# The memory's norm in a PSUM bank, and the low part of a unit of weights in one GpSimd operation

## What is computed

```python
def layer_norm(x, g, b):
    mu = jnp.mean(xf, -1, keepdims=True)
    var = jnp.mean(jnp.square(xf - mu), -1, keepdims=True)
    return ((xf - mu) * lax.rsqrt(var + LN_EPS) * g + b).astype(x.dtype)
...
mem_n = layer_norm(mem, mem_ln_g, mem_ln_b)
...
mk, mv = jnp.split(mem_n @ w_mem_kv[i], 2, axis=-1)
```

## Time and profile before

| what | value |
| --- | --- |
| median of 3 runs | 1919.36 us (1918.63 to 1919.83) |
| the profiled execution's own time | 1918.94 us |
| its span | 1917.1 us |
| TensorE (PE) busy | 1867.1 us, 97% |
| TensorE weight loads (PEld) | 1529.6 us, 80% |
| GpSimd (POOL) busy | 1517.8 us, 79% |
| ScalarE (ACT) busy | 945.5 us, 49% |
| VectorE (DVE) busy | 805.3 us, 42% |
| low parts on GpSimd (L1183) | 1242 operations, 1476.8 us |
| high parts on ScalarE (L1211) | 624 operations, 616.3 us |

### The profile page before, as it was taken

How to read it: one execution, slowest core, us unless ns; L and a number is a source line. 1 busy time by engine, 2 the same in 40 slices (tenths; PEclk the granted TensorE clock), 3 DMA queues, 4 the chain that set the end, 5 groups by cost and what they waited for, 6 DMA issues and landing times.

```text
span 1917.1 us, 27395 instructions
## 1 busy us (share of the span) xinstructions
PE 1867.1 (97%) x9610; PEld 1529.6 (80%) x9610; DVE 805.3 (42%) x1929; ACT 945.5 (49%) x1501; POOL 1517.8 (79%) x1330
## 2 busy tenths in 40 slices
PE   7999999999999999999999999999999999999999
PEld 6778888877888887788888678887787887788877
DVE  6784110446311155411146741106757445455534
ACT  3554444354444355444435644434656654555743
POOL 6768989884897977698987779797686887777785
PEclk9999999999999999999999999999999999999999
DMA  8454656563766554465655456655564564555453
GB/s 274 132 153 149 194 154 232 180 194 102 208 196 214 176 187 139 145 189 147 238 161 149 153 163 186 196 195 166 173 181 130 157 205 153 164 170 176 132 175 110
DMA packets 184557, 330.54 MB, mean 172 GB/s; under 512 B 12220, under 2 KB 44520, under 8 KB 184424
## 3 DMA queue, kind: packets, MB, share of 16 engines
q1 hardware_dynamic: 176512, 323.21, 54.4%
q10 hardware_dynamic: 7912, 5.59, 1.0%
HBM read 325.35 MB, written 3.41 MB: 171 GB/s over the span
## 4 chain that ended last, share of the span: by engine, by line
PE 84%; POOL 5%; DVE 5%; DMA 2%; ACT 2%; issue 2%; SPq 0%; DVEq 0%; ACTq 0%
PE acc L1417 24%; PE acc L1418 23%; PE acc L1424 21%; POOL w_lo L1183 5%; PE tps L1364 4%; PE acc L1439 2%; PE acc L1420 2%; PE ops L1481 2%; PE tps L1457 2%; DMA raw<-in_w_down 1%; PE acc L1388 1%; PE acc L1390 1%; PE acc L1389 1%; DVE QT L1594 1%; PE ops L1376 1%
## 5 line engine op out<-in xcount | busy, mean ns | idle before, releaser
L1183 POOL TENSOR_TENSOR w_lo<-raw,w_hi 128x512 fp32r<-128x512 f32 (+2 forms) x1242 | 1476.8, 1226 | 358.8 <-ACT w_hi L1211 357.4
L1211 ACT CAST w_hi<-raw 128x1024 fp32r<-128x1024 f32 (+3 forms) x624 | 616.3, 991 | 745.7 <-PE acc L1424 560.4
L1417 PE MATMUL acc<-w_hi,xT_hi 128*128 128x512 f32 (+1 forms) x1808 | 687.0, 384 | 4.9 <-ACT U L1245 3.0
L1418 PE MATMUL acc<-w_lo,xT_hi 128*128 128x512 f32 (+1 forms) x1808 | 667.5, 373 | 0.0
L1424 PE MATMUL acc<-w_hi,xT_lo 128*128 128x512 f32 (+2 forms) x1744 | 505.3, 371 | 0.0
L1417 PEld LDWEIGHTS acc<-w_hi,xT_hi 128*128 128x128 f32 x1808 | 341.8, 189 | 74.3 <-issue 14.5
L1418 PEld LDWEIGHTS acc<-w_lo,xT_hi 128*128 128x128 f32 x1808 | 342.4, 189 | 52.6
L1424 PEld LDWEIGHTS acc<-w_hi,xT_lo 128*128 128x128 f32 x1744 | 318.2, 189 | 58.4 <-DVE xT_lo L1694 1.2
L1754 DVE TENSOR_TENSOR H<-G,acc 128x512 f32<-128x512 f32 (+1 forms) x48 | 30.9, 643 | 332.7 <-PE acc L1424 332.7
L1417 PE MATMUL acc<-w_hi,hT_hi 128*128 128x512 f32 x352 | 139.6, 396 | 3.4 <-POOL w_lo L1183 3.4
L1418 PE MATMUL acc<-w_lo,hT_hi 128*128 128x512 f32 x352 | 137.3, 390 | 0.0
(11 more groups left out here) (209 smaller groups left out, 1998.8 us busy)
## 6 DMA issues: line engine op xcount, KB each, us to landing
raw<-in_w_gate_up SPq DMA_DIRECT2D x160, 512.0 KB, 4.0
raw<-in_w_in SPq DMA_DIRECT2D x104, 512.0 KB, 4.1
raw<-in_w_down SPq DMA_DIRECT2D x88, 512.0 KB, 4.1
raw<-in_w_out SPq DMA_DIRECT2D x48, 512.0 KB, 3.4
raw<-in_w_in_a SPq DMA_DIRECT2D x32, 512.0 KB, 3.9
raw<-in_w_in_b SPq DMA_DIRECT2D x20, 512.0 KB, 4.4
raw<-in_w_mem_kv SPq DMA_DIRECT2D x16, 512.0 KB, 4.1
raw<-in_w_gate_up SPq DMA_DIRECT2D x32, 256.0 KB, 2.8
```

Source lines behind the costliest of these rows:

```text
L1183: ins = nc.gpsimd.tensor_tensor(w_lo[:, r, i, 0:ch.width], raw[:, r, i, 0:ch.width], w_hi[:, slot, i, 0:ch.width].bitcast(F32), ALU.subtract)
L1211: nc.scalar.copy(w_hi[:, u.u % SPLIT, 0:u.nk, 0:u.chunk.width], raw[:, u.u % RAW, 0:u.nk, 0:u.chunk.width]).then_inc(S["hi_ready"], 1)
L1417: nc.tensor.matmul(o, hi[:, tok], wh, start=first_k, stop=False)
L1418: ins = nc.tensor.matmul(o, hi[:, tok], wl, start=False, stop=False)
```

## The change

Three things are edited.
- `low_part` on GpSimd: one operation over both k-tiles of the unit instead of one for each. It computes the same numbers, and raises the same semaphore once. The first unit's low part is made by VectorE, as before.
- The memory's norm: three operations for each half, through bank 1 of `ops`: `(m - mean) * r` into the bank, `* gain` in the bank, `+ bias` back into the rows. Before the first, VectorE waits for the release of the bank's last holder. The plan gives the task this room, and the half releases the bank itself.
- Costs in the plan: the low part 230 + 1.97 ns a column instead of 240 + 2.12 (for 1024 columns 2247 instead of 2411 ns), and a half of the memory's norm 2300 instead of 1600 ns.

```diff
             else:
-                u.low = self.task("POOL", "low", u, 240 + 2.12 * size, "lo_ready", [u.split])
+                u.low = self.task("POOL", "low", u, 230 + 1.97 * size, "lo_ready", [u.split])
...
                 one = p.stage(apply, fn, [gain.load, first, *also[t]], prio=t - 1 if fn == "rms_pre" else 0, half=half, **st)
                 halves.append(one)
+                if fn == "mem_norm":
+                    one.room, one.release, one.it.banks = ("ops", [(1,)]), one, [one]
...
-    norm_tiles("mem_norm", g, [[mem]] * T, "mem", scale=2500, acts="m")
+    norm_tiles("mem_norm", g, [[mem]] * T, "mem", scale=2500, apply=2300, acts="m")
...
                 pool.wait_ge(S["hi_ready"], u.split.n)
-                for i in range(u.nk):
-                    ins = nc.gpsimd.tensor_tensor(w_lo[:, r, i, 0:ch.width], raw[:, r, i, 0:ch.width],
-                                                  w_hi[:, slot, i, 0:ch.width].bitcast(F32), ALU.subtract)
-                ins.then_inc(S["lo_ready"], 1)
+                c = slice(0, ch.width)
+                nc.gpsimd.tensor_tensor(w_lo[:, r, 0:u.nk, c], raw[:, r, 0:u.nk, c], w_hi[:, slot, 0:u.nk, c].bitcast(F32),
+                                        ALU.subtract).then_inc(S["lo_ready"], 1)
...
                 elif fn == "mem_norm":
-                    m = rows("mem")[:, t, HALF[st.half]]
-                    norm_apply(t, m, m, halves(st.gain, st.half), done)
+                    m, (gg, bb) = rows("mem")[:, t, HALF[st.half]], halves(st.gain, st.half)
+                    mv, r = norm_columns(t, False)
+                    z = ops[:, st.banks[0].slot[0], :]
+                    for h in st.banks[0].held:
+                        dve.wait_ge(S[h.sem], h.n)
+                    link(v.tensor_scalar(z, m, mv[:, 0:1], r, ALU.subtract, ALU.mult))
+                    link(v.tensor_tensor(z, z, gg, ALU.mult))
+                    v.tensor_tensor(m, z, bb, ALU.add).then_inc(done, 1)
```

## The result

The changed kernel takes 1926.07 us (median of 6 runs, 1925.22 to 1927.53), the kernel before beside it 1919.59 (1917.43 to 1921.59): ratio 1.0036, interval [1.0023, 1.0049]. The profiled execution took 1925.97 us, its span 1924.1. The forecast was 1911.6, with 1905.0 to 1918.6: it missed on the far side; slower had been given a chance of 0.07.

What follows compares the result with a forecast made beforehand. TensorE, busy 97%, was taken as the bound, leaving its 50 us of standing to change. Terms -9.3 - 3.5 + 5 = -7.8 took 1918.94 to 1911.1; median 1911.6 us, range 1905 to 1918.6.

Steps and rivals of the forecast that it cites:

- Norm in a bank, -9.3: Memory's norm near 42 us: unheld bank operations let TensorE transpose earlier; 7.4 + 1.4 + 0.5 = 9.3 us gained.
- Low parts at the w_down starts, -3.5: At four w_down starts TensorE waits for low parts; merged units come 0.16 us sooner, 3.5 us gained, bounds 0 and 5.
- What the longer operation costs VectorE, +5: Held VectorE operations wait longer where VectorE leaves a GpSimd run early: 7.1 us at most, 5 taken.
- the list of places: Places said to cost: GpSimd runs at 1362.43, 1663.17 and 1681 us; 2.7 + 2.2 + 2.2 us at most.
- The condition of two tiles read from SBUF: From the norm's 8.76 us operation: a VectorE operation reading two SBUF tiles is held while GpSimd works.
- The price per hold: A held VectorE operation waits for 2.39 us of GpSimd instead of 1.30, up to 1.09 us more each.
- the argument of the run of fixed work: A GpSimd run is fixed work; operations held until its end finish as now, so longer operations add nothing there.
- the 450 us place: Two low parts at 450.57 us: the first held operation waits longer, the second not at all; they end as now.
- behind the latent: Six latent operations ahead of 1406 us grow up to 6.5 us, covered by idle VectorE; counted nothing, 2 if cover short.
- Order, 0 +- 3: New plan costs reorder all queues a little; no sign given, 3 us either way allowed.
- Rival 2: Every held operation on the path pays in full, 12 us in all, against gains of 12.8: 1918.6 us; chance 0.13.
- Rival 3: VectorE shut out through whole GpSimd runs at 1362, 1663, 1681 us and the latent: 22 us lost, 1928.5; chance 0.05.

Runs made afterwards that it cites:

- after: The changed kernel, with all three edits, measured beside the kernel before: 1926.07 us, ratio 1.0036.
- norm_one_op: Kernel before plus the norm in a bank and all low parts merged, in the order of the old low-part cost: 1918.45 us, ratio 0.9991.
- after_far: The changed kernel, its new order kept, with only the 34 units at held places split into two operations again: 1910.07 us, ratio 0.9952.
- one_op_far: norm_only with the low part merged for all units except the 34 at held places: 1903.02 us, ratio 0.9908.
- one_op_near: norm_only with the low part merged for only the 34 units at held places: 1925.59 us, ratio 1.0028.
- norm_only: The changed kernel with the old two-operation low part and its old plan cost, leaving the norm in a bank alone: 1909.73 us, ratio 0.9951.
- split_again: The changed kernel with the low part in two operations again, plan costs and order kept: 1914.76 us, ratio 0.9975.
- low_cost: The kernel before with only the plan's low-part cost changed to 230 + 1.97, so only the order differs: 1923.03 us, ratio 1.0017.
- one_low_op: The kernel before with only the low part merged into one operation, order unchanged: 1926.96 us, ratio 1.0037.

## Why the prediction was wrong

In terms of runs, the time of after is 1919.4 - 9.7 (norm) + 15.9 (long operation, 34 held units) - 6.7 (long operation, the others) + 7.6 (order, after against norm_one_op) = 1926.5; 1926.1 was measured. The last term is taken from after itself, so the sum tests only the three before it; for the order there is a second pair of runs, after_far against one_op_far, with 7.1. Against the forecast, the long operation brought 10.9 us more than its +5, the order 7.6 more than its 0, the low parts 3.2 more gain and the norm 0.4.

- **Norm in a bank, -9.3: right** (-9.7). So was its working: the first operation is not held, the transposes come early, the clock stays up. What was overlooked, that the w_mem_kv loads become the next to be late, costs 1.2 us here, and more in the new order (below).
- **Low parts at the w_down starts, -3.5: right in kind, a little small.** The 589 units outside the held places give 6.7, of which 5.6 are steps of 1.2 to 1.6 us at the four starts. A stretch of the chain like the earlier trace rows still goes through GpSimd in after (14.18 us, six operations).
- **What the longer operation costs VectorE, +5: the step that failed.** It measured 15.9. Two things were wrong with it. First, the list of places. It was made by looking for operations longer than the same form elsewhere; the two operations that end a top-k are held in both layers (1.14 and 1.53 us), so they had no shorter twin and were not seen. They are 7.2 of the 15.9 (steps of 3.7 and 3.5). The condition of two tiles read from SBUF was too narrow as well: the first of them reads one. Second, the price of a stand. I priced held time alone, 1.09 us a hold. But stands of 1.7 us or less grew to 2.35 and 4 us, and in one_op_near's trace TensorE's clock dropped for some microseconds after each: 1.4 to 1.7 us at each of the four places (the second top-k's end has 0.58 over 1068 to 1072 us). For the mixed maps 7.1 was the most I allowed at three places, with 0.9 for one more; they measured 4.1, 2.7 and 0.9, together 7.7 where 5 was taken. The price per hold itself was right (1.1 us each, in the rows of the top-k and of the small columns), and so, nearly, was the argument of the run of fixed work: the 450 us place moved 0.7 us, the nine small operations end with GpSimd's run in both, and behind the latent the steps show 0.5 us at most.
- **Order, 0 +- 3: the second step that failed, too small an allowance.** It is +3.6 on the kernel before, +5.0 with the norm in the bank and split low parts, +7.6 and +7.1 with long ones (all, or all but the 34). With the norm quick, the largest part lies at 45 to 52 us, a step of 4.9 between norm_only and split_again: in the new order TensorE waits 3.1 us for QT at 53 us, and the clock is 0.70 over 52 to 56. In after it waits twice, and the windows show its clock:

```profile
44.00:48.00 4.00, 1.54 (x5) 1.30 (x6) 3.36 (x11) 2.87 (x5) 4.00 (x2) 0.91 0.48 146
48.00:52.00 4.00, 4.00 (x13) 3.14 (x12) 3.82 (x8) 0.93 (x2) 4.00 (x4) 0.67 0.00 0
```

  The first of the two waits, 2.6 us for a low part, hangs on a load that takes longer here:

```profile
28.71 14.09 DMA raw<-in_w_mem_kv
```

  The plan's figure for a low part was made smaller, which is true of GpSimd, but the plan knows neither of the held operations nor of loads that wait behind one another. That the load is the cause in this order is read from the chain alone; no run moved it there. The steps of the order elsewhere, of 1 to 3 us, plus and minus, were not followed, so most of why this order is worse stays open.
- **The rivals.** Rival 2 (every held operation pays in full, 1918.6) was nearest in kind, and lacked the top-k ends, the clock and the order. Rival 3 gave 1928.5, near the result, but by starvation through whole runs; in after the mixed maps' operations each end with one GpSimd operation, so that its number is near is luck. The rule of the Trainium skill that rival 2 went by, "SBUF — State Buffer", "Who interferes with whom" (the shared port pair is held for a whole instruction and the other engine is blocked), was the better guide: the three lengths of hold above agree with it. It doesn't explain the 8.76 us of the earlier trace rows, of which nothing more was learned: the same hold is there in low_cost (8.30 us) and in one_low_op (7.31) too.

## What to carry to other kernels

Merging small GpSimd operations saves their fixed part only where GpSimd is waited for, and makes each VectorE operation that waits for one of them wait longer: in this kernel it paid to merge where VectorE had nothing that another engine waits for, and to split finely where it had. To find the held places, don't compare an operation with its like alone, since one that is always held has no free twin; compare its end with the ends of GpSimd's operations. And price a longer TensorE stand with what it may do to the clock: where the clock fell here, 1.4 to 1.7 us came on top of the waiting itself. And a plan's cost made truer can give a worse order: measure the order by itself.

## What the runs showed of the hardware that was not expected

- The clock after a short TensorE stand differs from case to case. Stands of 1.62 us (norm_one_op, near 45 us) and 1.74 (norm_only, 1675 us) left the granted clock at 1.00, and those of 1.9, 2.35, 2.6, 3.1 and 4 us shown or named above were followed by windows of 4 us at 0.57 to 0.82. But the length of the stand does not settle it. In one_low_op the stand of 2.35 us at the first top-k's end is followed by 1.00:

```profile
124.01 1.07 PE L1363 MATMUL tps<-ident,U 128*128 128x128 f32 x8 [2.35 <-DVE U L1632]
122.00:126.00 4.00, 1.99 (x18) 1.89 (x20) 3.96 (x10) 0.12 (x1) 2.81 (x2) 1.00 0.36 119
126.00:130.00 4.00, 4.00 (x29) 2.94 (x28) 3.00 (x7) 3.76 (x11) 3.00 (x3) 1.00 0.42 136
```

  and in one_op_far a stand of 1.67 us by 0.57:

```profile
1650.74 0.55 PE L1466 MATMUL tps<-ident,L 128*128 128x128 f32 x3 [1.67 <-DVE L L2019]
1652.00:1656.00 4.00, 4.00 (x20) 3.61 (x20) 2.30 (x5) 3.17 (x15) 1.06 (x1) 0.57 0.02 9
```

  Each trace is one execution. Whether the same stand costs the same in every execution of a kernel was not tried.
- A hold ends with the GpSimd operation that runs, at all three lengths, even in a run without gaps: sixteen operations of 256 columns in 11.43 us let a VectorE operation in after each of eleven. What held L1594 through seven operations at 32.38 is still open.
